# A v projection in seven block products, with weight sums on GpSimd

## The reference

```
h = RMSNorm(x);  p = h @ W_in          # columns: conv h|B|C (512 each), q, k (256), v (512), g (512), gate_low (16)
y_conv = B * causal_conv3(C * h_c)
log_a = log_sigmoid(gate_low @ W_up + b) / 16;  b = cumsum(log_a) within chunks of 64 tokens
q_dec = q*exp(b);  k_dec = k*exp(-b);  k_rem = k*exp(b_last - b)
o = masked(q_dec k_dec^T) v + q_dec @ state,  state <- decay*state + k_rem^T v       # 4 heads
x += concat(y_conv, RMSNorm(o) * silu(g)) @ W_out
x += top-4 of 32 experts (clamped SwiGLU, 1024 wide) of RMSNorm(x);  out = RMSNorm(x)
```

## Time and profile before

| what | us |
|---|---|
| median of three runs | 1022.5 |
| the profiled execution: its own time | 1022.29 |
| its span on the core | 1020.5 |
| TensorE (PE) busy | 998.2 (98%) |
| VectorE (DVE) busy | 279.8 (27%) |
| ScalarE (ACT) busy | 149.7 (15%) |
| GpSimd (POOL) busy | 10.8 (1%) |
| bytes moved | 423.87 MB, mean 415 GB/s |

### The profile page before, as it was taken

How to read it: one execution, slowest core, us unless ns; L and a number is a source line. 1 busy time by engine, 2 the same in 40 slices (tenths; PEclk the granted TensorE clock), 3 DMA queues, 4 the chain that set the end, 5 groups by cost and what they waited for, 6 DMA issues and landing times.

```text
span 1020.5 us, 12891 instructions
## 1 busy us (share of the span) xinstructions
PE 998.2 (98%) x5032; PEld 412.6 (40%) x5032; DVE 279.8 (27%) x685; ACT 149.7 (15%) x302; POOL 10.8 (1%) x29
## 2 busy tenths in 40 slices
PE   9999999999999999999999999999999999999997
PEld 7799733333333333333333333333333333333334
DVE  2888522222212221222221222212221222122122
ACT  2311311111111111111111111111111111111112
POOL 1010000000000000000000000000000000000000
PEclk9999999999999999999999999999999999999999
DMA  9986999999999999999999999999999999999996
GB/s 367 423 338 255 406 374 420 428 426 433 430 430 430 432 432 432 432 432 432 432 432 432 432 432 432 432 432 432 432 430 432 432 432 432 426 429 428 425 423 262
DMA packets 25526, 423.87 MB, mean 415 GB/s; under 512 B 3096, under 2 KB 3744, under 8 KB 7456
## 3 DMA queue, kind: packets, MB, share of 16 engines
q1 hardware_dynamic: 24480, 422.10, 97.3%
q10 hardware_dynamic: 1024, 1.47, 0.4%
HBM read 422.51 MB, written 1.05 MB: 415 GB/s over the span
## 4 chain that ended last, share of the span: by engine, by line
PE 80%; DMA 18%; issue 1%; DVE 0%; ACT 0%; SPq 0%; POOL 0%; ACTq 0%; PEldq 0%; DVEq 0%; POOLq 0%
PE bank L1858 33%; PE bank L1879 19%; DMA ring<-in_w_expert 14%; PE bank L1508 5%; PE bank L1717 5%; PE y L1922 5%; DMA ring<-in_w_down_last 4%; PE bank L1897 3%; PE y L1658 2%; PE bank L1793 1%; PE bank L1500 1%; PE bank L1976 1%; PE bank L1561 1%; PE bank L1903 1%; PE bank L1658 1%; DMA g_h<-in_x_cols 1%
## 5 line engine op out<-in xcount | busy, mean ns | idle before, releaser
L1858 PE MATMUL bank<-ring,x_t 128*64 128x512 f32 x1984 | 447.3, 597 | 0.2 <-DVE x_t L1321 0.2
L1858 PEld LDWEIGHTS bank<-ring,x_t 128*64 128x64 f32 x1984 | 134.2, 137 | 262.8 <-issue 259.6
L1879 PE MATMUL bank<-ring,act 128*64 128x512 f32 x960 | 223.0, 596 | 7.4 <-DMA ring<-in_w_expert 7.4
L1361 DVE TENSOR_TENSOR gu_b<-bank,bias_t 128x512 f32<-128x512 f32 x64 | 44.3, 692 | 323.8 <-PE bank L1897 323.7
L1879 PEld LDWEIGHTS bank<-ring,act 128*64 128x64 f32 x960 | 66.3, 137 | 133.5 <-issue 133.5
L827 ACT COPY gu_sb<-bank 128x512 f32<-128x512 f32 x64 | 37.4, 585 | 222.7 <-PE bank L1858 222.7
L1314 DVE TENSOR_TENSOR x_t<-bank,cols 128x512 f32<-128x512 f32 x30 | 20.8, 692 | 165.1 <-PE bank L1793 165.1
L1922 PE MATMUL y<-z,p_t 64*128 64x512 f32 x240 | 59.6, 615 | 0.0
L1717 PE MATMUL bank<-x_sb,p_row 128*64 128x512 f32 x248 | 58.5, 592 | 0.0
L1300 DVE TENSOR_SCALAR p_row<-slot,rank,rstd 128x64 f32<-128x64 f32 x62 | 16.6, 310 | 147.6 <-PE bank L1903 147.6
L831 ACT ACTIVATE act<-gu_b 128x256 f32<-128x256 f32 x62 | 25.8, 416 | 192.2 <-DVE gu_b L1367 192.2
(11 more groups left out here) (275 smaller groups left out, 536.6 us busy)
## 6 DMA issues: line engine op xcount, KB each, us to landing
ring<-in_w_expert SPq DMA_DIRECT2D x66, 4096.0 KB, 30.7
ring<-in_w_expert SPq DMA_DIRECT2D x46, 2048.0 KB, 17.0
ring<-in_w_expert SPq DMA_DIRECT2D x14, 1024.0 KB, 9.0
ring<-in_w_in SPq DMA_DIRECT2D x4, 2048.0 KB, 26.4
ring<-in_w_down_last SPq DMA_DIRECT2D x6, 1024.0 KB, 37.9
ring<-in_w_out SPq DMA_DIRECT2D x2, 2048.0 KB, 27.4
ring<-in_w_expert SPq DMA_DIRECT2D x8, 512.0 KB, 5.7
ring<-in_w_in SPq DMA_DIRECT2D x2, 1024.0 KB, 13.5
```

Source lines behind the costliest of these rows:

```text
L1361: dve.tensor_tensor(gu_b[:, :, :, :], bank[2][:, :].rearrange("p (f a s) -> p a f s", a=2, f=4), bias_t[:, :, 4 * h:4 * h + 4, ds(e, 1)] . ...
L1858: ins = mm(bank[h][a * SLOTS:(a + 1) * SLOTS, :], x_t_of(it)[:, k, :], w[:, kk, a, :], start=k == 0, stop=k == KT - 1)
L1879: ins = mm(bank[0][a * SLOTS:(a + 1) * SLOTS, :], act_of(it)[:, k, :], w[:, kk, a, :], start=k == 0, stop=k == KT - 1)
```

## The change

v becomes seven block products of four matmuls with 256 columns (multiply_v), in banks 3, 6, 7 and 4 of PSUM. Its sums:

- of h: four on VectorE right after h (x_sums), unscaled; the token's norm is still applied at the end.
- of weights: the difference v_diff on VectorE; three (v_sum, then block (0,0), then block (0,1)) on GpSimd, each waiting for the one before and for the product that still reads the block.
- of products: ScalarE copies four (keep_v_part), VectorE adds four quadrants into v_row, and ScalarE then scales v_row in place by the norms.

The gate projection's sum_1 and sum_3 move from VectorE to GpSimd, behind s_cs (their target w_sum shares memory with the decays' inputs). scale_h(0) moves ahead of the decays' log on VectorE, and scale_h(1) waits for the last v product. sum_2(0) comes after all four h_sums. The load of the second half of W_out waits for the last v product, as before for the last of v.

```diff
@@ gpsimd, after the constants
+            pool.wait_ge(s_v0, 16)
+            pool.wait_ge(s_slot[mix_slot(VV)], 16)
+            pool.tensor_tensor(v_sum[:, :, :], v_block(1, 0), v_block(1, 1), ALU.add).then_inc(s_sum, 1)
+            pool.wait_ge(s_sum, 1)
+            pool.wait_ge(s_ts, 5)
+            pool.wait_ge(s_pj, V_PRODUCTS[1])
+            pool.tensor_tensor(v_block(0, 0), v_sum[:, :, :], v_block(0, 0), ALU.subtract).then_inc(s_sum, 1)
+            pool.wait_ge(s_sum, 2)
+            pool.wait_ge(s_pj, V_PRODUCTS[2])
+            pool.tensor_tensor(v_block(0, 1), v_block(0, 1), v_block(0, 0), ALU.subtract).then_inc(s_sum, 1)
+            pool.wait_ge(s_slot[mix_slot(BLOCKED[0])], 16)
+            pool.wait_ge(s_cs, 1)
+            pool.tensor_tensor(w_sum[:, :, :], w_block(0, 1, 0), w_block(0, 1, 1), ALU.add).then_inc(s_sum, 1)
+            pool.wait_ge(s_sum, V_SUMS + 1)
+            pool.tensor_tensor(w_block(0, 1, 0), w_block(0, 0, 0), w_block(0, 1, 0), ALU.subtract).then_inc(s_sum, 1)
@@ scalar
-            keep_v(3)
+            keep_v_part(0, 1, v_a)
+            keep_v_part(2, 4, v_d)
+            keep_v_part(1, 3, v_c)
 ...                                   # the three exponentials
-            keep_v(4)
+            keep_v_part(3, 5, v_a)
+            act_e.wait_ge(s_diag, TT + QUADS)
+            for t in range(TT):
+                act_e.activation(v_row[:, t, :], v_row[:, t, :], ACT.Copy, scale=rstd[:, t:t + 1]).then_inc(s_pk, 1)
@@ vector, after h, and after the two diagonals
+            dve.tensor_tensor(x_sums[:, 0, :, :], h_block(0, 1), h_block(0, 0), ALU.subtract).then_inc(s_ts, 1)
+            dve.tensor_tensor(x_sums[:, 1, :, :], h_block(1, 1), h_block(0, 1), ALU.subtract).then_inc(s_ts, 1)
+            dve.tensor_tensor(x_sums[:, 2, :, :], h_block(1, 1), x_sums[:, 0, :, :], ALU.subtract).then_inc(s_ts, 1)
+            dve.tensor_tensor(x_sums[:, 3, :, :], h_block(1, 0), x_sums[:, 2, :, :], ALU.subtract).then_inc(s_ts, 1)
+            dve.wait_ge(s_v0, 16)
+            dve.tensor_tensor(v_diff[:, :, :], v_block(0, 0), v_block(1, 0), ALU.subtract).then_inc(s_ts, 1)
@@ vector, between the biased gate and the log
+            scale_h(0)
@@ vector, after k_rem
-            scale_h(0)
-            sum_1(0)
-            sum_3(0)
+            dve.tensor_tensor(v_rows(0, 0), v_b, v_parts[:, 0, :], ALU.add).then_inc(s_diag, 1)
+            link(dve.tensor_tensor(v_parts[:, 1, :], v_parts[:, 1, :], v_parts[:, 2, :], ALU.add))
+            dve.tensor_tensor(v_rows(1, 1), v_parts[:, 3, :], v_parts[:, 1, :], ALU.add).then_inc(s_diag, 1)
             scale_h(1)
 ...                                   # h_sums 0 and 1
+            dve.tensor_tensor(v_rows(1, 0), v_d, v_parts[:, 3, :], ALU.add).then_inc(s_diag, 1)
+            dve.tensor_tensor(v_rows(0, 1), v_c, v_parts[:, 3, :], ALU.add).then_inc(s_diag, 1)
 ...                                   # h_sums 2 and 3
             sum_2(0)
             sum_4(0)
@@ tensor
-            project_v(0, range(2))
+            multiply_v(v_a, h_block(0, 0), v_block(0, 0), True, False)
 ...                                   # the gate's up projection
-            project_v(0, range(2, KT))
-            project_v(1, range(KT))
+            multiply_v(v_b, h_block(1, 0), v_block(0, 1), True, True)
+            multiply_v(v_d, x_sums[:, 1, :, :], v_diff, True, False)
+            pe.wait_ge(s_sum, 1)
+            multiply_v(v_c, x_sums[:, 0, :, :], v_sum, True, False)
+            pe.wait_ge(s_sum, 2)
+            pe.wait_ge(s_pk, 1)
+            multiply_v(v_a, x_sums[:, 2, :, :], v_block(0, 0), False, True)
+            multiply_v(v_d, x_sums[:, 3, :, :], v_block(1, 1), False, True)
+            pe.wait_ge(s_sum, 3)
+            multiply_v(v_c, h_block(1, 1), v_block(0, 1), False, True)
```

More of the change, by code:

```diff
@@ L52 @@
 PRODUCTS, SUMS, PARTS, QUADS = 7, 4, 4, 4
+V_SUMS = 3
 FIRST, SECOND = PRODUCTS * len(BLOCKED), PRODUCTS * (len(BLOCKED) + 1)
@@ L264, in build @@
         o_sq = y_t[:, 0:CT, :]
-        junk = at("junk", [P, D], slot_at(9))
+        junk = at("junk", [P, 2, D], slot_at(9))
+        v_diff = at("v_diff", [P, 4, 2 * P], slot_at(9) + 4096)
+        v_parts = at("v_parts", [P, PARTS, 2 * P], slot_at(9) + 12288)
+        x_sums = at("x_sums", [P, 4, 4, P], 8192)
+        v_sum = at("v_sum", [P, 4, 2 * P], 16384)
         diag = at("diag", [P, TT, P], slot_at(9) + 2 * 4096)
@@ L331, in build @@
         s_pj = sem("projected")
-        s_pk = sem("v_kept")
+        s_pk = sem("v_parts_and_rows_kept")
         s_pkd = sem("projection_scaled")
-        s_diag = sem("rstd_diagonal_ready")
+        s_diag = sem("rstd_diagonals_and_v_quadrants_ready")
         s_bc = sem("rstd_spread")
@@ L427, in build @@
         s_pool = sem("pool_step")
-        PROJ = [(QK, 0), (QK, 1), ("gk", 0), (VV, 0), (VV, 1)]
+        PROJ = [(QK, 0), (QK, 1), ("gk", 0)]
+        V_PRODUCTS = {product: len(PROJ) + 1 + i for i, product in enumerate((1, 2, 4, 3, 5, 6, 7))}
         TURN_BANK = ((0, 3), (5, 6))
@@ L441, in w_block, with v_block, v_rows @@
             return chunk_view(BLOCKED[c], KT)[:, 4 * half:4 * half + 4, 2 * P * m:2 * P * (m + 1)]
+        def v_block(m, half):
+            return chunk_view(VV, KT)[:, 4 * half:4 * half + 4, 2 * P * m:2 * P * (m + 1)]
+        def v_rows(m, t):
+            return v_row[:, t, 2 * P * m:2 * P * (m + 1)]
         def h_block(half, t):
@@ L458, in build @@
         out_a, out_b, out_c, out_d = ([bank[i][:, 0:2 * P] for i in banks] for banks in ((5, 1), (6, 4), (7, 7), (4, 2)))
+        v_a, v_b, v_c, v_d = (bank[i][:, 0:2 * P] for i in (3, 6, 7, 4))
         acc_a, acc_b, acc_c, acc_d = (bank[i][:, 0:2 * P].rearrange("p (a t) -> p a t", a=2) for i in (1, 2, 3, 0))
@@ L487, in _ @@
                 if c >= MIX_SLOTS:
-                    sp.wait_ge(s_pj, PROJ.index((c - MIX_SLOTS, 1)) + 1)
+                    sp.wait_ge(s_pj, PROJ.index((QK, 1)) + 1 if c == MIX_SLOTS else V_PRODUCTS[7])
                 src = w_in[c - 1] if c < WO else w_out[c - WO]
@@ L707, in _ @@
             act_e.wait_ge(s_x[0], 16)
-            square_sum(0, junk[:, :])
+            square_sum(0, junk[:, 0, :])
             act_e.wait_ge(s_x[1], 16)
-            square_sum(1, y_t[:, 0:4, :].rearrange("p k t -> p (k t)"))
+            square_sum(1, junk[:, 1, :])
             for t in range(TT):
@@ L716, in _, with keep_v_part @@
             act_e.dma_start(br_bc[:, :], b_router.partition_broadcast(P)[:, 0, :]).then_inc(s_late, 16)
[L718 to L721, removed]
+            def keep_v_part(p, product, src):
+                act_e.wait_ge(s_pj, V_PRODUCTS[product])
+                act_e.copy(v_parts[:, p, :], src).then_inc(s_pk, 1)
             act_e.wait_ge(s_gkb, 1)
@@ L952, in _ @@
                     dve.tensor_scalar(h_t[:, k, :], h_t[:, k, :], g_mix[:, k:k + 1], None, ALU.mult).then_inc(s_h, 1)
+            dve.wait_ge(s_h, KT)
+            dve.tensor_tensor(x_sums[:, 0, :, :], h_block(0, 1), h_block(0, 0), ALU.subtract).then_inc(s_ts, 1)
+            dve.tensor_tensor(x_sums[:, 1, :, :], h_block(1, 1), h_block(0, 1), ALU.subtract).then_inc(s_ts, 1)
+            dve.wait_ge(s_ts, 1)
+            dve.tensor_tensor(x_sums[:, 2, :, :], h_block(1, 1), x_sums[:, 0, :, :], ALU.subtract).then_inc(s_ts, 1)
+            dve.wait_ge(s_ts, 3)
+            dve.tensor_tensor(x_sums[:, 3, :, :], h_block(1, 0), x_sums[:, 2, :, :], ALU.subtract).then_inc(s_ts, 1)
             dve.wait_ge(s_cols, 16)
@@ L975, in scale_h @@
             def scale_h(t):
-                dve.wait_ge(s_pj, PROJ.index((VV, t)) + 1)
+                dve.wait_ge(s_pj, V_PRODUCTS[(2, 7)[t]])
                 c = slice(t * P, (t + 1) * P)
@@ L992, in sum_2 @@
             def sum_2(c):
-                dve.wait_ge(s_sum, SUMS * c + 1)
+                dve.wait_ge(s_sum, V_SUMS + SUMS * c + 2)
                 dve.wait_ge(s_prod, PRODUCTS * c + 1)
@@ L998, in sum_4 @@
             def sum_4(c):
-                dve.wait_ge(s_sum, SUMS * c + 3)
+                dve.wait_ge(s_sum, V_SUMS + SUMS * c + 3)
                 dve.wait_ge(s_prod, PRODUCTS * c + 2)
@@ L1061, in _ @@
             dve.tensor_tensor(k_rem[:, :, :], qk[:, 1, :, :], e_rem[:, :, :], ALU.mult).then_inc(s_dec, 1)
-            scale_h(0)
-            sum_1(0)
-            sum_3(0)
+            dve.wait_ge(s_pk, 1)
+            dve.wait_ge(s_pj, V_PRODUCTS[2])
+            dve.tensor_tensor(v_rows(0, 0), v_b, v_parts[:, 0, :], ALU.add).then_inc(s_diag, 1)
+            dve.wait_ge(s_pk, 4)
+            link(dve.tensor_tensor(v_parts[:, 1, :], v_parts[:, 1, :], v_parts[:, 2, :], ALU.add))
+            dve.tensor_tensor(v_rows(1, 1), v_parts[:, 3, :], v_parts[:, 1, :], ALU.add).then_inc(s_diag, 1)
             scale_h(1)
@@ L1068, in _ @@
             dve.tensor_tensor(h_sums[:, 1, :, :], h_block(1, 1), h_block(0, 1), ALU.subtract).then_inc(s_ts, 1)
+            dve.wait_ge(s_pj, V_PRODUCTS[6])
```

(46 more changed lines are left out.)

## The result

The changed kernel takes 1028.08 us (median of 4 runs, 1027.25 to 1029.15) against 1022.84 us of the kernel before (4 runs): ratio 1.0054, 95% interval 1.0041 to 1.0066. It is slower by some 5 us, 0.5%. The profiled execution took 1027.41 us, with a span of 1025.6 us against 1020.5.

The account below looks back on a forecast made before the run. TensorE's mixer work was taken to bound it, by releasing the expert-weight stream: 1022.29 + 4.7 (late transposes) + 0.8 (slow clock) = 1027.8 us profiled, 1028.0 us as median. Own range 1025 to 1030.5, with rivals 1020.6 to 1030.5 us.

Parts of the forecast that it names:

- v's seven products: In the mixer, v's matmuls on TensorE go from 13.74 us to 12.09 us, 1.65 us saved.
- What lies beside other work: Four x_sums, v_diff and scale_h(0) on VectorE and ScalarE's small copies fit into idle time, at no cost.
- A GpSimd sum: Each 128x1024 sum on GpSimd takes 2.2 us by itself, with 1.22 and 3.29 us as bounds.
- Turns: VectorE instructions with two SBUF inputs and GpSimd sums reading SBUF exclude each other whole; transposes start 4.7 us late.
- When it began: GpSimd's v_sum starts at 21.95 us, as v's second half lands; s_cs comes at 32.95 us instead of 29.06.
- The slow pace: TensorE, after standing 6.3 us before the transposes, may run at half clock: 0 to 1.7 us lost, 0.8 taken.
- The end: The experts' weight stream's last break waits for TensorE, so a shift in the mixer moves the end by the same amount.
- the prediction's own sign: Other steps are wrong if transposes' start to expert 0's first matmul, 92.2 us, changes, or the end doesn't follow that matmul.
- The first rival: No exclusion, or VectorE always first: k_rem ends near 31.8 us, v's saving is won, 1020.8 us; chance 0.30.
- The short exclusion: A GpSimd sum holds VectorE for only 1.2 to 1.7 us: 1022.5 to 1024.8 us, typically 1023.5; chance 0.11.
- Turns of 2.5 us and more: Third v sum and the gate's sums also late for TensorE, up to 10 us: over 1030.5 us; chance 0.05.

## Why the prediction was right

It forecast 1028.0 us; 1028.08 was measured. That close a hit is luck: the four runs spread from 1027.25 to 1029.15 us, and the profiled one took 1027.41, for which the forecast was 1027.8. By its steps:

- **v's seven products, 1.65 us.** They start 1.73 us apart; where nothing stood in the way, in the run with memsets, it is 1.63 us less from v's first matmul to the x_t copy named below than in the trace before (21.00 to 125.83 us against 20.08 to 126.54). Right.
- **What lies beside other work.** x_sums and v_diff hid as forecast: the chain starts v at 19.90 us, the kernel before at 20.24. (The fourth x_sum took 1.05 us instead of 0.69, beside a mask of GpSimd's; VectorE was to be idle there.)
- **A GpSimd sum, 2.2 us.** 2.35 to 2.38 alone. The figure in the Trainium skill, GPSIMD Engine Reference, section 3.1 (estimate 2.25 us), is a little nearer.
- **Turns.** The places and the order were those of the prediction: the third v sum before the log, the gate's first before q_dec, its second before k_dec. The log stood 2.14 us, q_dec 1.59 (forecast 1.4), k_dec 2.13 (2.2). Each ended 0.54 to 0.56 us after the sum that it stood for, a little less than the 0.69 us that it takes alone; in the same way the first mask of the earlier trace rows ended 0.42 us after L996, though it takes 0.657 alone.
- **When it began.** The prediction took v's second half to land at 21.9 us, as in the trace before. In this execution it was there by 19.8, so the sums ran some 2 us earlier, scale_h(0) stood 0.22 us instead of 1.75, and s_cs came at 30.9 instead of 32.95 us. From there to the end of k_rem it took 6.4 us, as forecast (37.3 instead of 39.4 us). The transposes came 2.5 us late (forecast 4.7), and TensorE stood 4.5 us (6.3).
- **The slow pace.** The term was 0.8 us, the middle of 0 and 1.7. It measured 2.34 us (2.12 of it the clock's), over its upper end: that bound was from 3.3 us of work at the start, and here the lower clock was granted until 42 us, for over 4 us of work. That the start ran at half pace, though PEclk prints 1.00, was read rightly: 38 records of the same form took 4.40 us in the run that kept TensorE busy, 0.116 us each against 0.235.
- **The end.** 2.52 + 2.34 = 4.86 us is what expert 0's first matmul was late, and the end followed it. From the x_t copy ahead of that matmul to the end of the span it is 894.0 us before (126.54 to 1020.5), 894.2 after (131.41 to 1025.6) and between 893.5 and 894.2 in all six experiments. By the prediction's own sign, the stretch from the transposes to expert 0's first matmul has changed, from 92.2 to 94.5 us; all of it is the 2.34 us behind the wait, the term that was too small.

So the sum was right partly by luck: the lateness of the transposes was taken 2.2 us too large, some 2 us of it through the landing, and the slow pace 1.5 us too small. The mechanism, its place and the sign were right. The bounds of the forecast's own range don't quite follow from their terms (1022.5 + 3.3 = 1025.8 and 1022.5 + 6.0 + 1.7 = 1030.2 us, not 1025 and 1030.5); the forecast doesn't hang on that.

The first rival (no exclusion) fell: GpSimd's sums were indeed in time for TensorE, but that wasn't what counted. The short exclusion fell too: a sum held VectorE for up to 2.14 us, not for 1.2 to 1.7. Only copies of one input in their place hold it for less than that (0.64, 0.26 and 0.83 us). Turns of 2.5 us and more didn't come: a sum takes 2.35 to 2.38 us alone, and TensorE waited for none. That the rule in the Trainium skill, SBUF — State Buffer, section "Who interferes with whom", holds for reads and not for writes is what the runs with copies and with memsets show (k_dec 1.52 us against 0.69).

Open: why v's second half lands earlier in one execution than in another, and why v itself starts earlier. GpSimd's first instruction on it began between 19.80 and 22.14 us in the traces of the changed kernel and the six experiments; the changed kernel's has the earliest of them, and the earliest start of v. How much of the 5 us varies with that isn't shown; its four runs lie within 1.9 us.

## What to carry to other kernels

Work given to GpSimd is not free for VectorE: while GpSimd read SBUF, the VectorE instructions with two inputs in SBUF stood here until that instruction was done, so count a sum of 2.4 us as up to 2.4 us of VectorE's chain, twice what VectorE would need for it (1.22 us). GpSimd instructions that only write (memsets) held nothing up. Put work that reads only beside VectorE's waits and its reads of PSUM, and look at the chain that VectorE carries there, not at its busy share. When an edit makes TensorE stand for some microseconds, price the slower clock behind it as well (2.1 us behind 4.5 us of standing here, nothing behind 2.5).

## What the hardware showed beside that

- Standing for 4.5 us brought the granted clock down to 0.50 while TensorE still stood, and 2.12 us were lost by it behind the wait; with matmuls on constants in the gap it stayed 1.00. In the run with quarter sums TensorE stood for 2.51 us and the granted clock stayed 1.00; the product right behind took 1.99 us, the next one 1.89.
- A copy of 128x512 from SBUF to SBUF, with one input, stood as well beside GpSimd's pieces: 0.85 us instead of 0.43. It is not only two inputs that make VectorE give way. No run here tells what sets it apart from the instructions with one input in PSUM, such as the scaling of q and k (L1018, 1.28 us for two, the same beside the first v sum as alone).
